# Thirty small groups of products moved next to their neighbours, and one copy ahead of an exponential, in a two-block transformer kernel

## What is computed

```
# first block
qkv, gate, gdn_qkv, gdn_gate, a, b, merge = split(rms_norm(x) @ w_in)
# stick-breaking attention, 8 heads of 64, blocks of 128 queries
z = q k^T * scale
log_keep = where(causal, -softplus(z), 0)
a = exp(log_sigmoid(z) + exclusive suffix sum of log_keep);  o_sb = (a @ v) * silu(gate)
# gated delta rule, 4 heads of 128, chunks of 64: a triangular solve, then a walk over states
u, w = solve(I + strict(beta * k k^T * decay), [v * beta, k * beta * exp(g)])
for each chunk: v_new = u - w S;  o = q S + intra v_new;  S = S * exp(g_last) + k^T v_new
x = x + rms_norm((sigmoid(merge) * o_sb w_sb + sigmoid(merge) * o_g w_gdn) @ w_out)
# second block
differential attention (4 double heads, softmax minus lambda * softmax) and
forgetting attention (8 heads, softmax with a cumulative forget bias), then w_out_2, then the MLP
x = x + rms_norm(relu(h @ w_up)^2 @ w_down)
```

## Time and profile before

| | us |
|---|---|
| median of 3 runs | 1095.16 |
| lowest, highest | 1094.94, 1095.47 |
| the profiled execution, whole time | 1094.89 |
| its span, first to last instruction | 1093.6 |
| of it PE busy | 1081.6 |
| DVE, ACT, POOL busy | 540.4, 567.8, 435.8 |

### The profile page before, as it was taken

The page is one execution under the profiler, slowest core; times in us unless marked ns, Lnnn a source line. Parts: engine busy times, 40 slices in busy tenths (PEclk is TensorE's granted clock), DMA queues, the critical chain, the costliest instruction groups (busy, mean ns, idle before and its releaser), DMA issues.

```text
span 1093.6 us, 14878 instructions
## 1 busy us (share of the span) xinstructions
PE 1081.6 (99%) x5669; PEld 886.6 (81%) x5669; DVE 540.4 (49%) x1151; ACT 567.8 (52%) x1082; POOL 435.8 (40%) x236
## 2 busy tenths in 40 slices
PE   8999999999999999999999999999999999999998
PEld 8877878778887788888778777789888888888886
DVE  3739789788765224142445455535111115544444
ACT  6555767767777642353556566554222224333333
POOL 4334342342532444553142332345444446444441
PEclk9999999999999999999999999999999999999999
DMA  9133121221322332723222321222333334323312
GB/s 259 48 96 88 42 75 39 79 60 40 95 58 63 92 97 97 232 77 81 79 78 59 96 79 58 77 87 79 105 97 97 97 97 131 100 97 97 97 57 77
DMA packets 140530, 97.24 MB, mean 89 GB/s; under 512 B 9014, under 2 KB 125091, under 8 KB 140459
## 3 DMA queue, kind: packets, MB, share of 16 engines
q1 hardware_dynamic: 138728, 95.03, 29.6%
q10 hardware_dynamic: 1730, 1.25, 0.4%
HBM read 94.14 MB, written 2.91 MB: 89 GB/s over the span
## 4 chain that ended last, share of the span: by engine, by line
PE 90%; DVE 6%; ACT 2%; issue 1%; DMA 1%; SPq 0%; POOL 0%; ACTq 0%; DVEq 0%
PE bank L467 28%; PE bank L1189 14%; PE bank L1207 14%; PE bank L508 5%; PE bank L886 4%; PE bank L860 4%; PE bank L870 4%; PE bank L1220 2%; DVE bank L2008 1%; DVE multipliers L2006 1%; PE bank L482 1%; PE bank L682 1%; PE bank L1035 1%; PE bank L997 1%; PE bank L1017 1%
## 5 line engine op out<-in xcount | busy, mean ns | idle before, releaser
L2469 POOL TENSOR_TENSOR ring<-raw_ring,ring 128x1024 fp32r<-128x1024 f32 x160 | 388.6, 2432 | 564.8 <-ACT ring L1234 564.8
L467 PE MATMUL bank<-hT,ring 128*128 128x512 f32 x1536 | 394.7, 402 | 0.5 <-ACT rawsb L1309 0.5
L467 PEld LDWEIGHTS bank<-hT,ring 128*128 128x128 f32 x1536 | 278.0, 188 | 57.9 <-issue 6.5
L1234 ACT CAST ring<-raw_ring 128x1024 fp32r<-128x1024 f32 x160 | 167.2, 1047 | 109.6 <-PE bank L1207 88.8
L1189 PE MATMUL bank<-hT,ring 128*128 128x512 f32 x672 | 152.5, 389 | 0.0
L1207 PE MATMUL bank<-ring,ring_u 128*128 128x512 f32 x672 | 152.5, 389 | 0.0
L1207 PEld LDWEIGHTS bank<-ring,ring_u 128*128 128x128 f32 x672 | 126.2, 188 | 26.2
L1189 PEld LDWEIGHTS bank<-hT,ring 128*128 128x128 f32 x672 | 126.1, 188 | 26.1
L2444 DVE TENSOR_TENSOR ring_u<-u,ring_u 128x1024 fp32r<-128x1024 f32 x32 | 80.7, 2529 | 73.8 <-ACT ring_u L1808 73.8
L2449 DVE TENSOR_TENSOR u<-u 128x512 f32<-128x512 f32 x32 | 22.9, 714 | 138.8 <-ACT u L1815 138.8
L1815 ACT ACTIVATE u<-bank 128x512 f32<-128x512 f32 x32 | 19.1, 598 | 114.8 <-PE bank L1189 108.3
(11 more groups left out here) (293 smaller groups left out, 1488.4 us busy)
## 6 DMA issues: line engine op xcount, KB each, us to landing
raw_ring<-in_w_in SPq DMA_DIRECT2D x144, 256.0 KB, 3.3
raw_ring<-in_w_up SPq DMA_DIRECT2D x64, 256.0 KB, 3.2
raw_ring<-in_w_down SPq DMA_DIRECT2D x64, 256.0 KB, 2.8
raw_ring<-in_w_out SPq DMA_DIRECT2D x32, 256.0 KB, 2.8
x<-in_x SPq DMA_DIRECT2D x8, 512.0 KB, 5.1
raw_ring<-in_w_branch_sb SPq DMA_DIRECT2D x8, 256.0 KB, 2.9
raw_ring<-in_w_branch_gdn SPq DMA_DIRECT2D x8, 256.0 KB, 3.3
cum<-cums SPq DMA_DIRECT2D x4, 512.0 KB, 5.3
```

What stands on the lines that cost most here:

```text
L467: p = pe.matmul(bank, m.slab_k8(n % 4)[:, a, k, :], m.hT[:, b, k, :], start=term == 0, stop=term == 23)
L1234: act.copy(m.ring[:, q, 0, :], m.raw_ring[:, q, :]).then_inc(s.slab_hi[q], 1)
L2469: pool.tensor_tensor(m.ring[:, q, 1, :], m.raw_ring[:, q, :], m.ring[:, q, 0, :].bitcast(F32), ALU.subtract).then_inc(s.slab_lo[q], 1)
```

## The change

On PE the change moves small groups, by a few wide products each, to where another small group stands, three times over in each of the two loops. On ACT the log part and the exponential of the stick gate are separate functions, and the copy of level 5 stands between them in the three looped heads; in the fourth head their order is as before. No operation is added or removed, and no DMA is moved.

```diff
@@ first block, PE, i in range(3) @@
         delta_decay(i)
-        tiles.to(24)
+        tiles.to(28)
         stick_v_rows(i)
-        tiles.to(28)
         stick_weights_T(i, 0, 0)
         stick_weights_T(i, 1, 0)
-        tiles.to(33)
+        tiles.to(34)
         stick_z(i, 1)
-        tiles.to(35)
         delta_v_rows(i)
-        tiles.to(47)
+        tiles.to(48)
         delta_gram(i)
-        tiles.to(50)
         stick_weights_T(i, 1, 1)
         stick_weights_T(i, 0, 1)
...
         delta_level_first(i, 5)
-        tiles.to(109)
         stick_weights_T(i, 1, 2)
         stick_weights_T(i, 0, 2)
...
         delta_solve(i)
         tiles.to(147)
-        stick_weights_T(i, 1, 3)
         delta_chunk(i, 0)
-        tiles.to(152)
-        stick_weights_T(i, 0, 3)
         tiles.to(153)
         delta_from_state(i, 1)
+        stick_weights_T(i, 1, 3)
+        stick_weights_T(i, 0, 3)
         tiles.to(155)
         delta_chunk(i, 1)
@@ second block, PE, i in range(3) @@
-        tiles.to(31)
+        tiles.to(34)
         fox_rows_T(i, 0, 0)
-        tiles.to(34)
         fox_rows_T(i, 1, 0)
-        tiles.to(51)
+        tiles.to(54)
         diff_rows_T(i, 1, 0, pairs)
-        tiles.to(54)
         diff_rows_T(i, 0, 0, pairs)
         fox_z(i, 1)
-        tiles.to(58)
+        tiles.to(62)
         diff_av(i, 1, 0, pairs)
-        tiles.to(63)
         diff_av(i, 0, 0, pairs)
         fox_rows_T(i, 1, 1)
         fox_rows_T(i, 0, 1)
...
-        tiles.to(86)
+        tiles.to(91)
         fox_rows_T(i, 0, 2)
-        tiles.to(91)
         fox_rows_T(i, 1, 2)
-        tiles.to(97)
         tiles.to(102)
...
         diff_av(i, 1, 1, pairs)
-        tiles.to(122)
         fox_rows_T(i, 0, 3)
         tiles.to(128)
@@ first block, ACT @@
+    def stick_gate_log(i):
+        log_of_sigmoid(sgate, m.rawsb[:, 3, :], s.sbg_sig, 4 * i)
+
     def stick_gate(i):
-        log_of_sigmoid(sgate, m.rawsb[:, 3, :], s.sbg_sig, 4 * i)
         exponential(sgate, s.sbg_dve, 2 * i + 1, s.sbg_sig)
...
         stick_exp(i, 2)
+        stick_gate_log(i)
+        delta_level(i, 5)
         stick_gate(i)
-        delta_level(i, 5)
```

## The result

| | before | after |
|---|---|---|
| median, us | 1095.22 | 1110.60 |
| lowest, highest | 1094.94, 1095.47 | 1108.75, 1110.76 |
| the profiled execution, whole time | 1094.89 | 1108.75 |
| its span | 1093.6 | 1107.4 |

The ratio is 1.0137, 95% interval [1.0125, 1.0149]: slower by 15.4 us. Forecast were 1107.5, and at most 1109.0. The direction and the places are as predicted, the size isn't: the median lies 1.6 us above the range. The four executions aren't alike. The profiled one has a mean granted clock of 0.998 and a span of 1107.4; the three others have 0.995 and spans of 1109.2 to 1109.4.

What follows compares the result with a forecast made beforehand. The prediction took PE, busy for 99% of the span, to bound the kernel. It summed 1094.9 + 5.4 (first loop) + 7.2 (second loop) = 1107.5 us, range 1097 to 1109, its own case at chance 0.45.

Steps and rivals of the forecast that it cites:

- (1): First loop: gram products one wide product later (+0.23, less 0.02) make DVE's long chain 0.21 us late.
- (2): First loop, at the solve: PE arrives at 188.9 and must wait to 189.27.
- (3): First loop: POOL's subtraction 0.4 us early, slow L1897 ends 0.4 sooner, first state's copy ends at 194.05, for 194.35.
- (4): First loop, delta_from_state(1): PE waits for the copy, eight transposes now stand behind it; 0.5 us a pass lost.
- (5): First loop, third state: POOL's subtraction gets ahead of DVE's times (L1901), so PE waits for L2046; +1.3 us a pass.
- (6): Second loop: fox_rows_T(0,0) three wide products later holds ACT's queue by 0.26 us; costs nothing, without slack 0.1.
- (7): Second loop: fox_rows_T(0,3) right behind diff_av(1,1) comes before its rows are scaled; +0.25 us a pass.
- (8): Second loop: diff_av(1,0) later puts POOL 0.03 us ahead of DVE's L2338, so fox_rows_T(1,1) waits; +2.15 a pass.
- rival A: Only the first loop's collision of DVE and POOL, DVE winning the second loop's close one: 1101.1 us; chance 0.27.
- B: Rival: only the second loop's collision of DVE and POOL: 1103.6 us; chance 0.07.
- C: Rival: no collision in either loop, slower by PE waiting for DVE alone: 1097.2 us; chance 0.11.
- D: Rival: not slower, DVE's chain doesn't hold delta_from_state and ACT's gain is kept: 1092.9 us, or 1092.3; chance 0.10.

Runs made afterwards that it cites:

- e13: e1 with DVE's level 6 subtraction ahead of the last soft's two subtractions, and three merges: 1093.13 us, ratio 0.9982.
- e12: e1 with PE's solve at wide product 146 in place of 144, and four merges: 1097.29 us, ratio 1.0021.
- e1: The kernel before with ACT's edit alone, PE's order untouched: 1094.45 us, ratio 0.9995.
- e6: The changed kernel with eight transposes (stick_weights_T) back ahead of delta_from_state(1): 1103.37 us, ratio 1.0077 to the kernel before.
- e9: The changed kernel with both the edits of e5 and e6: 1095.54 us, ratio 1.0005 to the kernel before.
- e10: The changed kernel with e5's exchange and DVE's times(qT) moved right behind least(XT): 1097.12 us, ratio 1.0020 to the kernel before.
- e5: The changed kernel with DVE's L2331 ahead of its copy of diff_av's six products: 1100.96 us, ratio 1.0055 to the kernel before.
- e3: The kernel before with PE's moves of the second loop alone: 1103.72 us, ratio 1.0083.
- e4: The changed kernel with diff_av(1,0) back at wide product 58 and diff_av(0,0) at 63: 1100.97 us, ratio 1.0054 to the kernel before.
- e15: The kernel before with PE waiting for POOL's subtraction ahead of diff_av(0,0)'s last four instructions, stall 2.20 us: 1104.20 us, ratio 1.0082.
- e16: The kernel before with PE waiting for POOL's subtraction ahead of all of diff_av(0,0), stall 2.85 us: 1105.03 us, ratio 1.0093.
- e7: The kernel before with PE's fox_rows_T(1,1) also waiting for POOL's subtraction, stall 1.76 us: 1099.92 us, ratio 1.0045.
- e2: The kernel before with ACT's edit and PE's moves of the first loop: 1100.45 us, ratio 1.0049.
- e11: The kernel before with an added PE wait in diff_av(0,0) that was never issued: 1095.33 us, ratio 1.0001.
- e14: The kernel before with PE waiting for POOL's subtraction ahead of diff_av(0,0)'s last two instructions, stall 1.98 us: 1100.97 us, ratio 1.0056.

## Why the prediction was right in its places and wrong in its size

- **The merging, 0.3 us for thirty groups.** Right in kind, a bit small: 0.10 a pass for three merges in e13 and 0.3 in the second loop of e12, 0.03 a merge where I took 0.01 of a range of 0.01 to 0.03.
- **ACT's edit, 1.7 us come free (3 x 0.56).** Right: L625's wait went, and e13 keeps 0.56 a pass. e1 kept 0.17, since 0.38 went to the solve.
- **(1) and (2), DVE's chain 0.21 late and a wait at the solve.** The wait was there (0.27 in the trace, released by L2024). e6 and e9 show that (1) to (3) cost nothing net: ACT's 0.56 pays for it.
- **(3) and (4), the state's copy sets PE's time.** Right to 0.03 us (194.08 for 194.05). Cost 0.57 a pass in e10, forecast 0.5.
- **(5), the collision at `times`.** Right: 1.29 a pass, forecast 1.3. The margin had looked safe at 0.4 and was 0.46. First loop: 5.5, forecast 5.4.
- **(6), nothing.** Right: no wait of PE for the moved rows' results.
- **(7), 0.25 a pass.** Measured 0.15 (48.26 for 48.11 in e5).
- **(8), the close one: POOL ahead by 0.03.** Right: it came in all three passes here, in all three of e3 and in all three of e6. But that it came true was luck, as far as its ground goes. "In the earlier trace rows 0.04 was enough" speaks of L1901, and e1 has that very pair at 0.04 with DVE not held; in all executions where it was recorded at 0.030 to 0.038 DVE kept its 0.68 (below, in the last section). Read so finely, the row that the step leaned on would have spoken for rival A at 0.03. L2331 is another kind of instruction. The trace before the change shows that POOL can hold it (at 685.81 us L2338 starts 1.90 behind a subtraction of POOL, lasts 0.67 and ends 0.16 after it), and has no race of it as close as this. The cost with the clock whole is 2.12 a pass, forecast 2.15. Rivals A, B, C and D fall; e4 and e5 are rival A made real, at 1101.0, where it had 1101.1.
- **The step that failed is the sum behind (8)**, "3 x (0.25 + 2.15) = +7.2", and with it "above 1109 little". A stall of PE was priced as the time it stands, and what the clock does behind it had no term in the sum. Behind a stall of 2.15 us the granted clock fell in some of the passes, and each time the work behind it lasted 1.5 us more (1.53 here, 1.58 and 1.65 behind the stalls of e15 and e16). In the profiled execution that was once: 1107.2 + 1.5 = 1108.7. The median's 1.9 us more go with a clock of 0.995 for 0.998; only their spans and mean clocks are on record, so that they hold a second stretch is argued from that, not seen. e5's 9.6 us are 6.4 and 3.2 in this way. A range to 1112 would have carried it: three stretches of 1.5 on top of 1107.5.

The rule of the Trainium skill that the prediction cited, an exclusive lock between the two engines, from "SBUF — State Buffer", section "Who interferes with whom", fits in sign and in size: in the two collisions here L1894 and L2331 end 0.56 and 0.15 after POOL's instruction does, so they ran when it was done. As the prediction words it, for two inputs in SBUF, it covers L1894, which reads two tiles; L2331 reads one tile and a column of factors (`b<-b,stat`), and that it is held too is what its row shows (2.47 for 0.34, in nine passes of nine here, in e3 and in e6), with nothing here that tells why.

**What stays open.** In one execution the clock falls behind one stall and not behind another of the same length and with the same work around it. No run here tells what decides. Also open is whether the stall of 1.98 never has it: these are five executions.

## What to carry to other kernels

Where PE is the bound, a merge of small groups was worth 0.03 us here, and one race that it turned cost 2.12: before moving one, write down which instruction of DVE like L1894 or L2331 (two tiles, or one tile and a column of factors, all in SBUF) stands within half a microsecond of each POOL instruction, and on which side. Such a race can be mended in either queue. In the second loop one exchange on DVE (e5) and PE's old order (e4) did the same, 1100.96 and 1100.97; in the first the exchange on DVE left 0.57 a pass (e10), since PE still came too early to the first state, and the transposes back in their place left nothing (e6). And work that is to fill a wait has inputs of its own (e12); price a stall that PE didn't have before with the clock behind it as well as with its length.

## What the runs showed of the hardware

The race between DVE and POOL isn't read off from their recorded starts alone. `times` at the end of the third head is recorded 0.030 to 0.046 us behind POOL's subtraction in seventeen profiled executions. In eight of them (the changed kernel, e1, e6, e7, e12, e13, e15, e16; 0.030 to 0.040) it keeps its 0.68 and POOL lasts 2.96 to 2.98 in place of 2.39; in the nine others (before, e2, e3, e4, e5, e9, e10, e11, e14; 0.039 to 0.046) it lasts 2.90. For this pair the recorded distance does sort them, but for the five at 0.039 and 0.040: DVE won all six at 0.030 to 0.038 and lost all six at 0.043 to 0.046. Yet L2331, another kind of instruction, is held in nine of nine at 0.024 to 0.031 (three passes each of the changed kernel, e3 and e6). So without rows of the same pair a forecast within some 0.05 us is a toss, and the loser pays over 2 us, if it is DVE, or 0.6, if it is POOL.

The clock: stalls of 1.48, 1.76 and 1.98 us left the granted clock whole in the profiled executions and moved no time beyond their length in the others; behind stalls of 2.15 to 2.85 it was at 0.52 to 0.71 over a few microseconds in some passes, with wide products 0.427 apart for 0.228, the lower of the two levels (1.2 GHz for 2.4) over part of such a stretch. It fell soon after PE had resumed, and not always at the same distance: at the second stall of e16 products that are 0.11 apart at the higher level are 0.21 apart from 0.2 us behind the resumption on, at the first only the wide products from 1.4 us on are slow. The Trainium skill, "TensorE: Matmul & The Clock Gate", section "What's actually happening", says that the array's clock passes a gate with a half and a full setting, by how busy the engine has been of late. The windows of this case agree with two levels; they show too that the low stretch can be longer than the stall that it follows: a granted clock of 0.62 over 3.6 us, as a mix of a half and a full clock, is 2.7 us at the lower level (an estimate), behind a stall of 2.15.
